# A selective scan on one Trainium2 core: every second C.B and state product goes to the transposes' PSUM bank

## What is computed

```
cum = jnp.cumsum(dt_c * a_neg, axis=2)
decay_end = jnp.exp(cum[:, :, -1:] - cum)
states = jnp.einsum('bcjgn,bcjgh,bcjghp->bcghpn', b_c, decay_end, dtx)
chunk_decay = jnp.exp(cum[:, :, -1])
h = h * chunk_decay + state              # from chunk to chunk
decay_in = jnp.exp(where(causal, seg, -inf))
cb = jnp.einsum('bcign,bcjgn->bcijg', c_c, b_c)
y_diag = jnp.einsum('bcijg,bcijgh,bcjghp->bcighp', cb, decay_in, dtx)
y_off = jnp.einsum('bcign,bcghpn,bcigh->bcighp', c_c, h_prev, jnp.exp(cum))
y = y_diag + y_off
```

## Time and profile before

| | us |
|---|---|
| median of 3 executions | 1487.65 |
| lowest, highest | 1486.85, 1488.76 |
| the profiled execution, its own time | 1478.55 |
| its span, first to last instruction | 1476.8 |
| TensorE busy in the span | 1366.5 (93%) |
| VectorE, ScalarE, GpSimd busy | 596.2, 395.3, 153.9 |
| mean granted TensorE clock | 0.983 of full speed |

### The profile page before, as it was taken

How to read it: one execution, slowest core, us unless ns; L and a number is a source line. 1 busy time by engine, 2 the same in 40 slices (tenths; PEclk the granted TensorE clock), 3 DMA queues, 4 the chain that set the end, 5 groups by cost and what they waited for, 6 DMA issues and landing times.

```text
span 1476.8 us, 29256 instructions
## 1 busy us (share of the span) xinstructions
PE 1366.5 (93%) x12461; PEld 823.0 (56%) x12461; DVE 596.2 (40%) x1095; ACT 395.3 (27%) x979; POOL 153.9 (10%) x182
## 2 busy tenths in 40 slices
PE   5999888999988999998999989999999999989876
PEld 2344444454544488754666555688757765555432
DVE  4365666456454664643222212242364532211112
ACT  3322333443434210220222212223162302211111
POOL 0000113122231200000011111000000001111100
PEclk9999999999999999999999999999999999999988
DMA  9655344434440451435999999967321369999993
GB/s 350 213 173 175 110 143 147 139 115 143 143 143 29 114 143 58 170 118 179 368 385 391 383 379 387 354 242 236 107 92 55 107 248 393 390 395 398 400 405 141
DMA packets 131495, 334.50 MB, mean 227 GB/s; under 512 B 13283, under 2 KB 63259, under 8 KB 125211
## 3 DMA queue, kind: packets, MB, share of 16 engines
q1 hardware_dynamic: 121851, 309.18, 57.5%
q0 software_dynamic: 6208, 12.60, 2.5%
q10 hardware_dynamic: 3296, 10.73, 2.0%
HBM read 325.79 MB, written 14.81 MB: 231 GB/s over the span
## 4 chain that ended last, share of the span: by engine, by line
PE 68%; SPq 17%; DMA 5%; DVE 5%; issue 3%; ACT 2%; ACTq 0%; DVEq 0%; POOLq 0%
SPq L592 12%; PE ps L1253 11%; PE ps L1611 9%; PE ps L1270 7%; PE ps L1504 6%; PE ps L1650 5%; PE ps L1561 4%; SPq L594 4%; DMA ring<-in_moe_w_down 3%; PE ps L1197 3%; PE ps L1672 2%; PE ps L1930 2%; PE ps L1840 2%; PE ps L1345 2%; PE ps L1358 1%
## 5 line engine op out<-in xcount | busy, mean ns | idle before, releaser
L1253 PE MATMUL ps<-aT,ring 128*128 128x512 f32 x384 | 174.9, 603 | 3.3 <-DMA dskip<-in_ssd_d 3.3
L1611 PE MATMUL ps<-ring,ssb 128*32 128x256 f32 x2256 | 132.5, 386 | 11.2 <-DMA ring<-in_moe_w_up 9.9
L2454 DVE COPY big<-ps 32x256 f32<-32x256 f32 x162 | 68.6, 423 | 148.7 <-PE ps L1650 147.0
L1611 PE MATMUL ps<-tmp,ssb 128*32 128x256 f32 x1984 | 114.7, 383 | 9.6 <-DMA tmp<-in_moe_w_up 9.6
L2445 DVE TENSOR_TENSOR ssb<-ssb,ps 128x128 f32<-128x128 f32 (+1 forms) x56 | 19.5, 348 | 256.6 <-ACT ssb L1017 256.6
L1253 PEld LDWEIGHTS ps<-aT,ring 128*128 128x128 f32 x384 | 70.6, 191 | 86.2 <-issue 81.3
L1270 PE MATMUL ps<-aT,ring 128*128 128x512 f32 x256 | 114.2, 595 | 0.0
L1611 PEld LDWEIGHTS ps<-ring,ssb 128*32 128x32 f32 x2256 | 74.4, 112 | 65.0 <-DMA ring<-in_moe_w_up 18.3
L1650 PE MATMUL ps<-ring,ssb 128*32 128x256 f32 x1648 | 96.7, 386 | 6.2 <-DMA ring<-in_moe_w_down 5.6
L1030 ACT COPY big<-ps 32x256 f32<-32x256 f32 x162 | 58.8, 363 | 144.3 <-PE ps L1650 142.8
L1611 PEld LDWEIGHTS ps<-tmp,ssb 128*32 128x32 f32 x1984 | 66.2, 110 | 54.1 <-DMA tmp<-in_moe_w_up 9.2
(11 more groups left out here) (438 smaller groups left out, 1954.7 us busy)
## 6 DMA issues: line engine op xcount, KB each, us to landing
ring<-in_ada_w SPq DMA_DIRECT2D x44, 1024.0 KB, 8.5
ring<-in_moe_w_down SPq DMA_DIRECT2D x40, 1024.0 KB, 18.2
ring<-in_moe_w_gate SPq DMA_DIRECT2D x56, 512.0 KB, 9.8
ring<-in_moe_w_up SPq DMA_DIRECT2D x56, 512.0 KB, 13.1
tmp<-in_moe_w_gate SPq DMA_DIRECT2D x48, 512.0 KB, 12.4
tmp<-in_moe_w_up SPq DMA_DIRECT2D x48, 512.0 KB, 16.8
ring<-in_ssd_in_w SPq DMA_DIRECT2D x20, 1024.0 KB, 7.4
tmp<-in_moe_w_down SPq DMA_DIRECT2D x16, 1024.0 KB
```

The lines of the kernel that those rows point to most:

```text
L1253: ins = pe.matmul(ps[:, bank, :], slot(u)[:, k, (i % 2) * P:(i % 2 + 1) * P], aT[:, k, :], start=(k == 0), stop=(k == KD - 1))
L1611: ins = pe.matmul(tiled_gu[32 * c:32 * c + 32, 2 * h + i, :].rearrange("p (r n) -> p r n", r=2), XgT[l][:, k * C + 32 * g:k * C + 32 * g + ...
L2454: ins = dve.tensor_copy(Y[s % 2][32 * g:32 * g + 32, 256 * c:256 * c + 256], tiled_y[32 * c:32 * c + 32, 2 * h + i, :])
```

## The change

`shared_banks()` gives every use of bank 4 a bank (`BANK4`), the number of takes of `s_b4v` that it waits for (`BEFORE4`), and for those in bank 3 the number of takes of `s_b3v` (`B3_DONE`). In each step that has C.B or states ahead of R, uses 1 up to the number of early ones are marked `ahead`: they wait for one take fewer than before, that is for all but the use directly in front, and those with an odd number go to bank 3. In step 0 and the steps with n % 4 = 3 these are states 3 and 5 in bank 3, state 4 and R in bank 4. In the steps with n % 4 = 2 they are state 0 and the first R in bank 3, state 1 in bank 4; the second R of such a step is not marked. Every later transpose in bank 3 waits for the takes up to the last product that borrowed the bank (`B4_DONE`). The order of the instructions on each engine is as it was. Steps -1, 1, 4, 5, 8, 9 and 12 to 15 keep the banks and waits of their bank 4 uses.

```diff
+def shared_banks():
+
+    bank, before, b3_done, b4_done = {}, {}, {}, {}
+    turned, borrowed = len(bank3_uses(-1)), 0
+    for n in range(-1, STEPS):
+        uses = bank4_uses(n)
+        early = sum(use[0] != "R" for use in uses) if n >= 0 else 0
+        turned += len(bank3_uses(n)) if n >= 0 else 0
+        for use in bank3_uses(n):
+            b4_done[use] = borrowed
+        for i, use in enumerate(uses):
+            ahead = 1 <= i <= early
+            bank[use] = 3 if ahead and i % 2 else 4
+            before[use] = B4[use] - 1 if ahead else B4[use]
+            if bank[use] == 3:
+                b3_done[use], borrowed = turned, B4[use] + 1
+    return bank, before, b3_done, b4_done
+
+
+BANK4, BEFORE4, B3_DONE, B4_DONE = shared_banks()
...
-                    act.activation(Rex[d], ps[:, 4, :], ACT.Exp).then_inc(s_b4v, 1)
+                    act.activation(Rex[d], ps[:, BANK4["R", n, d], :], ACT.Exp).then_inc(s_b4v, 1)
...
             def bank3_free(use):
                 if B3[use]:
                     pe.wait_ge(s_b3v, B3[use])
+                if B4_DONE[use]:
+                    pe.wait_ge(s_b4v, B4_DONE[use])
...
             def bank4_free(use):
-                if B4[use]:
-                    pe.wait_ge(s_b4v, B4[use])
+                if BEFORE4[use]:
+                    pe.wait_ge(s_b4v, BEFORE4[use])
+                if use in B3_DONE:
+                    pe.wait_ge(s_b3v, B3_DONE[use])
...
-                pe.matmul(ps[:, 4, :], BK[:, t, :], wx[q % 2], start=True, stop=True).then_inc(s_b4, 1)
+                pe.matmul(ps[:, BANK4["st", g, q], :], BK[:, t, :], wx[q % 2], start=True, stop=True).then_inc(s_b4, 1)
```

More of the change, by code:

```diff
@@ L1296, in cb @@
                 for t in range(NT):
-                    ins = pe.matmul(ps[:, 4, t * P:(t + 1) * P], BT[:, g, t * P:(t + 1) * P],
+                    ins = pe.matmul(ps[:, BANK4["cb", g], t * P:(t + 1) * P], BT[:, g, t * P:(t + 1) * P],
                                     CT[:, g, t * P:(t + 1) * P], start=True, stop=True)
@@ L1314, in rows_per_head @@
                         c = g * HG + h + w
-                        ins = pe.matmul(ps[w * HP:(w + 1) * HP, 4, h * HP:(h + 2) * HP], pick[:, c:c + 1].to_broadcast([P, HP]),
+                        ins = pe.matmul(ps[w * HP:(w + 1) * HP, BANK4["R", n, d], h * HP:(h + 2) * HP], pick[:, c:c + 1].to_broadcast([P, HP]),
                                         cparts[:, d, t * P:(t + 1) * P], start=True, stop=True)
@@ L2106, in take_cb @@
                 dve.wait_ge(s_b4, B4["cb", g] + 1)
-                dve.tensor_copy(cbs[g % 2], ps[:, 4, :]).then_inc(s_b4v, 1)
+                dve.tensor_copy(cbs[g % 2], ps[:, BANK4["cb", g], :]).then_inc(s_b4v, 1)
             def take_state(g, q):
@@ L2114, in take_state @@
                     dve.wait_ge(s_b4, B4["st", g, q] + 1)
-                    dve.tensor_copy(H[d][0], ps[:, 4, :]).then_inc(s_b4v, 1)
+                    dve.tensor_copy(H[d][0], ps[:, BANK4["st", g, q], :]).then_inc(s_b4v, 1)
                 else:
@@ L2120, in take_state @@
                     dve.wait_ge(s_b4, B4["st", g, q] + 1)
-                    dve.tensor_tensor(H[d][n], H[d][n], ps[:, 4, :], ALU.add).then_inc(s_b4v, 1)
+                    dve.tensor_tensor(H[d][n], H[d][n], ps[:, BANK4["st", g, q], :], ALU.add).then_inc(s_b4v, 1)
             def take4(use):
```

## The result

The changed kernel takes 1475.82 us (median of four executions, 1475.09 to 1477.07) against 1488.20 of the kernel before beside it: 12.4 us less, ratio 0.9923 with a 95% interval of 0.990 to 0.9946. The forecast was 1475.4 within 1471.0 to 1480.5.

A forecast was written before the change was run, and what follows sets the result against it. TensorE was taken to bound the kernel, its scan waits being reducible. Terms 2.55 + 3.65 + 3.4 + 0.3 + 0.6 + 1.7 = 12.2 us took 1487.65 to 1475.4, range 1471.0 to 1480.5.

The forecast's parts named there:

- What bounds, and what the change reaches: In the scan, TensorE's waits at state products and R bound; the change addresses 14.5 us of them.
- Steps 0, 3 and 11: Scan steps with four states ahead of R: R comes sooner, gaining 3.65, 2.55 and 1.7 us.
- Steps 2 and 10: Scan steps with C.B, two states and two R: second R comes 1.7 us sooner in each, 3.4 in all.
- Steps 6 and 7: Scan steps with gate projections or a covered R: only the wait ahead of one state goes, 0.3 and 0.6 us.
- Added waits: 31 new waits on bank 3's takes and transposes: put at nothing, at most 1.6 us.
- The clock: Step 0, 195 to 199 us: TensorE's fall to 1.2 GHz, costing 1.54 us, should go with the stalls.
- nothing would change behind the scan: Time between the same instructions behind the scan should be unchanged.
- (a): Rival: VectorE, ScalarE and GpSimd pace the scan more than thought; only 6.0 us gained, 1481.6; chance 0.09.
- (b): Rival: same within 0.2%, an old shared-count wait remains or expert stages take the gain; 1485 to 1488; chance 0.07.
- (c): Rival: slower, shorter but more frequent pauses drop TensorE's clock in the scan, 1.54 us per fall; 1500.7; chance 0.04.
- The carry-over: Whole kernel: the 12.2 us scan gain reaches the end and carries from the profiled execution to the median, 1475.4.
- the last sign of being wrong: Forecast is wrong if the gain in the scan is over 9 us and the end shows under 6.

The follow-up runs named there:

- holding GpSimd back: Changed kernel with GpSimd's weighted x for states 2 and 3 held back until VectorE has finished mix: median 1473.97 us, ratio to before 0.9914.
- the half with three: Kernel before with new banks and waits only in steps 2, 6 and 10 (C.B, two states, two R): 1485.14 us, ratio 0.9976.
- the GpSimd edit: Changed kernel with GpSimd's last weighted x of a group ahead of add_squares: median 1474.54 us against 1476.58 for the changed kernel.
- the moved take: Changed kernel with VectorE's take of state 1 ahead of the second half of mix in steps 2, 6 and 10: median 1474.01 us.
- the second comparison: Changed kernel as it is, timed once more against the kernel before: 1476.58 us, ratio 0.9936.
- the half with four: Kernel before with new banks and waits only in steps 0, 3, 7 and 11 (four states ahead of R): 1479.60 us, ratio 0.9939.

## Why the prediction was right, and where it was off

*What bounds, and what the change reaches.* Right. The kernel with new banks and old waits shows that the gain hangs on the lifted waits and not on the bank. The waits of L1306 and L1315 for VectorE went from 17.6 us to 6.4 (forecast: about 5).

*Steps 0, 3 and 11.* 3.6, 2.5 and 1.65 us against 3.65, 2.55 and 1.7. In each the forecast named what comes next: the convolution and the exponents behind it (two waits of 0.47), `silu` ahead of the transposes, GpSimd's queue (1.67, forecast 1.4). The exponents and GpSimd's queue were each moved by an edit, and their waits went. The last weighted x of step 11 kept its long duration (1.50 us), as the forecast took it.

*Steps 2 and 10.* The term that was mis-sized: 1.7 forecast, 1.2 measured, each. I moved the take of state 1 by the 0.34 us of its chain's start and left the duration of `mix` as it was. But state 1 itself runs earlier, so GpSimd's next weighted x starts earlier and falls on the second half of `mix` (0.69 in step 2 of the kernel before, 1.41 now). Measured from C.B the take of state 1 therefore comes later, not sooner: 230.81 - 225.29 = 5.52 us, before 232.71 - 227.36 = 5.35. That is 0.17 later where the forecast had 0.34 sooner, and these 0.5 us are the whole difference in each step. What I should have asked is which work on the other engines the earlier product sets going. That the overlap is the cause is shown by holding GpSimd back.

*Steps 6 and 7.* 0.55 and 0.9 against 0.3 and 0.6. The difference is the overlap of matmuls that don't wait, about 0.2 in each (state 3 to state 4 of step 7 went from 2.11 to 1.30 us, and only 0.64 of that was idle time), which the forecast kept out of the sum.

*Added waits.* Put at nothing; the kernel with old waits agrees, to some 0.2 us of TensorE's time in the scan.

*The clock.* In all four traces in which the states of step 0 wait as before (both of the kernel before, the old waits, the half with three) TensorE slows down behind R of step 0, and in none of the nine others. So this fall hangs on the waits: TensorE needs 2.40 us from R to `y_off` in the changed kernel, 3.90 before. Not all of the 1.5 us are kept. TensorE is 3.0 + 1.5 = 4.5 us early at `y_off` and the transposes come 3.6 early; 0.9 is given back behind the exponents and `silu`, as the forecast had it. It named one place where the clock falls, and overlooked another: in all thirteen traces it also falls at the start, at about 175 us, where TensorE waits 3.1 us (2.95 in one) ahead of R. Elsewhere the forecast was too simple: it said that nothing would change behind the scan. Behind the last R of the scan the changed kernel ran at the lower level for some 3 us (stretches, columns as above):

```profile
465.00:470.00 5.00, 3.02 (x35) 1.70 (x35) 1.98 (x3) 2.70 (x7) 2.27 (x2) 1.00 0.00 0
470.00:472.00 2.00, 2.00 (x16) 1.67 (x13) 1.38 (x2) 1.24 (x3) 0.00 (x0) 0.53 0.00 0
472.00:474.00 2.00, 2.00 (x8) 1.24 (x7) 0.69 (x1) 0.13 (x1) 0.00 (x0) 0.61 0.00 0
```

It cost 1.6 us in this trace (8.48 us from the last R to the long run of gate projections, 6.87 without it). The stall ahead of it, 1.86 us, is the same in all traces. The fall came in six of thirteen (the changed kernel twice, its two halves, the GpSimd edit and the moved take), in no trace of the kernel before or of the old waits, and not in the other four with lifted waits. So the change doesn't always bring it. Whether the change makes it likelier these traces can't say: six of ten with lifted waits and none of three without are too few. What decides it stays open.

*The rivals.* (a) and (b) are ruled out by size. (c), the clock, is ruled out as well: one fall less in step 0, one more at times behind the last R. The rule of the Trainium skill, "TensorE: Matmul & The Clock Gate", section "A second HAM failure mode: psum-queue depth-cycling", by which going around PSUM banks makes the clock go up and down, isn't borne out where the banks were put to use: there the pauses grew shorter, and the clock between 185 and 465 us is full in both traces of the changed kernel.

*The carry-over.* 12.2 us on the median was right (12.4 and, in the second comparison, 10.1, each with some 3.5 us of uncertainty on either side), though the profiled execution went from 1478.55 to 1475.81 and not to 1466.3. That the first comparison agrees to 0.2 us is luck: the traces give 11.4, with steps 2 and 10 1.0 under the forecast and steps 6 and 7 about 0.5 over it. By the two profiles shown first the last sign of being wrong was met, over 9 us in the scan and 2.8 at the end. The later ones answer it: behind the last R the kernel before took 1004.3 us and the changed one 1005.0 and 1476.2 - 468.73 = 1007.5, against 997.9 in that one execution. A loss of up to some 3 us behind the scan can't be excluded by them.

## What to carry to other kernels

A second PSUM bank is worth the wait that it lets you lift, step by step, and each step is paid out only up to the next late thing on the other engines: walk the chain of takes, mixes and exponents once with the product at its earliest and read where it catches on. Ask also what the earlier product sets going on GpSimd, since that work may fall on VectorE's. Compare distances between the same instructions and not spans, when single executions differ by more than the effect.

## What was not expected

- GpSimd's operation on SBUF and VectorE's with two SBUF inputs stretch each other: the second half of `mix` 0.69 to 1.41 us, the weighted x 1.05 to 1.50. The Trainium skill, "SBUF — State Buffer", section "SBUF: two separate sides", calls it a lock between the two; the traces agree, in that a VectorE operation in the other's way takes about as long as what is left of the other plus its own 0.69. The second half of `mix` starts at 229.47, the second weighted x ends at 227.85 + 2.49 = 230.34: 0.87 + 0.69 = 1.56, measured 1.41.
- In the two halves of the change the clock fell once more each, both times behind stalls that this half had left as they were, and which had brought no fall in the kernel before: in the half with three early uses behind step 3 (23.56 us from R of step 3 to the next, 20.66 before: 2.9 us), in the half with four behind the first R of step 2, at 231 us (clock 0.60 and 0.55 over 4 us, 1.6 us). So the same stall is followed by a fall in one execution and not in another. That lifting stalls takes away chances for a fall is shown for step 0 alone. Stretches of the half with four (length, busy and instructions by engine, clock, DMA share, GB/s):

```profile
231.00:233.00 2.00, 1.93 (x16) 0.45 (x16) 1.93 (x4) 0.60 (x1) 0.32 (x1) 0.60 0.00 0
233.00:235.00 2.00, 2.00 (x26) 1.72 (x24) 1.68 (x3) 0.82 (x2) 0.00 (x0) 0.55 0.44 74
```
- Groups of 256 expert matmuls took 13.81 us in one execution of the kernel before and 14.06 to 14.42 in all others, at full clock from 713 to 726 us there and from 707 to 720 in the changed kernel.
